# Splitting merged's chunks between the last branch products, with memory's norm behind them

## The reference

```python
def first_block(x, ...):
    h = rmsnorm(x, norm_pre[l])
    u = h @ w_in[l]
    branches = (gdn_branch(...), gla_branch(...), ssd_branch(...), nsa_branch(...))
    gates = jax.nn.sigmoid(_cols(u, offs, 'merge_gate', 'merge_gate')).reshape(bsz, s_len, N_BRANCH, D_MODEL)
    merged = jnp.zeros((bsz, s_len, D_MODEL), F32)
    for n, y in enumerate(branches):
        merged = merged + gates[:, :, n] * (y @ w_br[l, n].astype(F32))
    out = merged.astype(x.dtype) @ w_out[l]
    x = x + rmsnorm(out, norm_post[l])
    return x

def second_block(x, mem, ...):
    ...
    x = x + memory_cross_attention(rms_norm(x, norm_mem_w[l]), rms_norm(mem, norm_memkv_w[l]),
                                   w_mq[l], w_mkv[l], mem_q_norm_w[l], mem_k_norm_w[l], w_mo[l])
```

## Time and profile before

| | us |
|---|---|
| median of 3 runs | 1944.07 |
| lowest, highest | 1939.2, 1944.46 |
| the profiled execution | 1942.46 |
| its span in the profile | 1939.4 |
| PE busy | 1863.8 |
| VectorE, ScalarE, POOL busy | 820.2, 662.7, 534.0 |
| mean granted clock of TensorE | 0.99 of 2.4 GHz |

### The profile page before, as it was taken

The page is one execution under the profiler, slowest core; times in us unless marked ns, Lnnn a source line. Parts: engine busy times, 40 slices in busy tenths (PEclk is TensorE's granted clock), DMA queues, the critical chain, the costliest instruction groups (busy, mean ns, idle before and its releaser), DMA issues. The chain is left out here.

```text
span 1939.4 us, 29067 instructions
## 1 busy us (share of the span) xinstructions
PE 1863.8 (96%) x11709; PEld 1370.5 (71%) x11709; DVE 820.2 (42%) x1692; ACT 662.7 (34%) x1417; POOL 534.0 (28%) x412
## 2 busy tenths in 40 slices
PE   6999999999999999998999998999999999999997
PEld 5789988888898666676878876987774444444443
DVE  4466565344322555533423255323343444333333
ACT  4543233332223555543343256444331111111110
POOL 2342143435543444273245231353200000000000
PEclk9999999999999999999999999999999999999999
DMA  5230122213132211152223221223529999999994
GB/s 165 67 91 25 45 61 93 75 44 109 55 96 82 74 34 44 44 202 98 85 87 107 69 97 23 88 87 116 211 94 378 414 415 413 421 423 417 420 423 173
DMA packets 132681, 313.40 MB, mean 162 GB/s; under 512 B 15280, under 2 KB 102080, under 8 KB 107968
## 3 DMA queue, kind: packets, MB, share of 16 engines
q1 hardware_dynamic: 132544, 311.49, 43.1%
HBM read 309.37 MB, written 2.10 MB: 161 GB/s over the span
## 5 line engine op out<-in xcount | busy, mean ns | idle before, releaser
L321 POOL TENSOR_TENSOR unit_low<-unit_ring,unit_high 128x512 fp32r<-128x512 f32 x332 | 437.3, 1342 | 771.6 <-ACT unit_high L314 771.5
L358 PE MATMUL dense<-hT,unit_high 128*128 128x512 f32 x560 | 228.8, 409 | 3.0 <-DVE dense_temps L531 1.7
L360 PE MATMUL dense<-hT,unit_low 128*128 128x512 f32 x560 | 219.7, 392 | 0.0
L359 PE MATMUL dense<-hT,unit_high 128*128 128x512 f32 x560 | 219.5, 392 | 0.0
L314 ACT CAST unit_high<-unit_ring 128x512 fp32r<-128x512 f32 x332 | 186.2, 618 | 32.3 <-PE dense L360 22.0
L451 PE MATMUL dense<-unit_high,hT 128*128 128x256 f32 x608 | 176.0, 289 | 0.7 <-POOL unit_low L321 0.4
L452 PE MATMUL dense<-unit_low,hT 128*128 128x256 f32 x608 | 172.0, 283 | 0.0
L453 PE MATMUL dense<-unit_high,hT 128*128 128x256 f32 x608 | 171.9, 283 | 0.0
L4295 DVE TENSOR_TENSOR x<-x,side 128x512 f32<-128x512 f32 x128 | 80.6, 682 | 115.5 <-PE side L4137 115.5
L358 PEld LDWEIGHTS dense<-hT,unit_high 128*128 128x128 f32 x560 | 106.0, 189 | 29.1 <-issue 3.6
L359 PEld LDWEIGHTS dense<-hT,unit_high 128*128 128x128 f32 x560 | 106.1, 190 | 23.6 <-issue 3.1
(11 more groups left out here) (606 smaller groups left out, 3642.2 us busy)
## 6 DMA issues: line engine op xcount, KB each, us to landing
expert_slot<-w_exp_gate SPq DMA_DIRECT2D x64, 1024.0 KB, 10.3
expert_slot<-w_exp_up SPq DMA_DIRECT2D x64, 1024.0 KB, 10.6
expert_slot<-w_exp_down SPq DMA_DIRECT2D x64, 1024.0 KB, 9.6
unit_ring<-w_in SPq DMA_DIRECT2D x55, 1024.0 KB, 5.2
unit_ring<-w_mkv SPq DMA_DIRECT2D x8, 1024.0 KB, 5.4
unit_ring<-w_br SPq DMA_DIRECT2D x14, 512.0 KB, 6.4
x<-x SPq DMA_DIRECT2D x8, 512.0 KB, 5.7
w_out_raw<-w_out SPq DMA_DIRECT2D x4, 1024.0 KB, 9.4
```

The costliest lines, as they stand in the source:

```text
L321: nc.gpsimd.tensor_tensor(low[:, at:at + 512], raw[:, at:at + 512], high[:, at:at + 512], ALU.subtract).then_inc(*self.split.up())
L358: nc.tensor.matmul(out, high[:, k, c], rh, start=(k == 0), stop=False)
L359: nc.tensor.matmul(out, high[:, k, c], rl, start=False, stop=False)
L360: last = nc.tensor.matmul(out, low[:, k, c], rh, start=False, stop=(k == kd - 1))
```

## The change

A new function `split_merged` holds one split of `merged`, as it stood in `output_projection`. It is now called from `blocks`: splits 0 and 1 ahead of product 4, 2 and 3 ahead of product 5, 4 ahead of product 6, 5 ahead of product 7, and 6 and 7 behind it. Memory's norm is written behind all eight. The load of `mix_gain` moves behind the reload of x on SP. Of the weights' rests, those whose number i is no multiple of three go to VectorE (ten of sixteen; POOL keeps 0, 3, 6, 9, 12 and 15), where the odd ones went before. Product 3 and gate 6 are written earlier between the pieces, product 3 ahead of piece 11 and not 12, gate 6 ahead of piece 13 and not behind the loop. PE's own order doesn't change.

```diff
+def split_merged(core, S, merged, k):
...
+        if k == 0:
+            act.wait_ge(*S.last_gate)
+        act.wait_ge(*S.merged_chunk[k])
+        nc.scalar.mul(hT[:, 0, k, :], merged[:, k, :], 0.5).then_inc(*scalars.up())
+    high = scalars.now()
...
+        dve.wait_ge(*high)
+        nc.vector.scalar_tensor_tensor(out=hT[:, 1, k, :], in0=merged[:, k, :], scalar=0.5, in1=hT[:, 0, k, :],
+                                       op0=ALU.mult, op1=ALU.subtract).then_inc(*vectors.up())
+    S.split[k] = vectors.now()
...
-def output_projection(core, ring, S, x, xin, merged, gain_row, w_high, w_low, temps, turn_memory, mem_keys):
+def output_projection(core, ring, S, x, xin, gain_row, w_high, w_low, temps, turn_memory, mem_keys, load_mix_gain):
...
-    for k in range(KD):
...
-            nc.scalar.mul(hT[:, 0, k, :], merged[:, k, :], 0.5).then_inc(*scalars.up())
...
-            nc.vector.scalar_tensor_tensor(out=hT[:, 1, k, :], in0=merged[:, k, :], scalar=0.5, in1=hT[:, 0, k, :],
-                                           op0=ALU.mult, op1=ALU.subtract).then_inc(*vectors.up())
-        split[k] = vectors.now()
...
     again = [s.now() for s in S.x_sems]
+    load_mix_gain()
...
-            if i in (0, 2, 5, 8, 12):
-                next(dense, None)
+            if i in (0, 2, 5, 8, 11, 13):
+                next(dense)
...
-            if i % 2:
+            if i % 3:
...
-        next(dense)
         wait_for(section.sync, [S.yT_ready, S.held_free[1]])
...
+        next(dense)
+
+        for chunks in ((0, 1), (2, 3), (4,), (5,)):
+            for k in chunks:
+                split_merged(core, S, merged, k)
+            next(dense)
         run(dense)
+        for k in (6, 7):
+            split_merged(core, S, merged, k)
         wait_for(section.scalar, [S.held_free[7]])
...
-        wait_for(section.sync, mem_ready[1:])
-        S.mix_gain_landed = load("mix_gain", (S.mix_gain[:], ins["norm_mix_w_2"].to_broadcast([P, D])))
...
+        def load_mix_gain():
+            wait_for(section.sync, mem_ready[1:])
+            S.mix_gain_landed = load("mix_gain", (S.mix_gain[:], ins["norm_mix_w_2"].to_broadcast([P, D])))
```

More of the change, by code:

```diff
@@ L775, in __init__ @@
         self.chunk, self.conv_out_free, self.merged_chunk, self.pool_chunk = {}, {}, {}, {}
+        self.split = {}
         self.reduced, self.x_done, self.root_ready, self.mem_heads_done = {}, {}, {}, {}
@@ L2383, in first_norm, with _ @@
     S.hT_ready = vectors.now()
-def output_projection(core, ring, S, x, xin, merged, gain_row, w_high, w_low, temps, turn_memory, mem_keys):
+def split_merged(core, S, merged, k):
+    nc, section, hT = core.nc, core.section, S.hT
+    vectors, scalars = core.sig("core_vectors"), core.sig("core_scalars")
+    @section.scalar
+    def _(act):
+        if k == 0:
[3 more added lines that the diff above has]
+    high = scalars.now()
+    @section.vector
+    def _(dve):
+        dve.wait_ge(*high)
[3 more added lines that the diff above has]
+def output_projection(core, ring, S, x, xin, gain_row, w_high, w_low, temps, turn_memory, mem_keys, load_mix_gain):
     nc = core.nc
@@ L2393, in output_projection @@
     rs = S.head_sums
-    last_gate, split = S.last_gate, {}
+    split = S.split
     part = S.out_part
@@ L2815, in blocks @@
         mem_keys = dense_mem_k(core, ring, S, memT, kT_mem)
-        output_projection(core, ring, S, x, xin, merged, post_gain, w_high, lambda k: w_low[:, k, :], temps, turn_memory, mem_keys)
+        def load_mix_gain():
+            wait_for(section.sync, mem_ready[1:])
+            S.mix_gain_landed = load("mix_gain", (S.mix_gain[:], ins["norm_mix_w_2"].to_broadcast([P, D])))
+        output_projection(core, ring, S, x, xin, post_gain, w_high, lambda k: w_low[:, k, :], temps, turn_memory, mem_keys, load_mix_gain)
         block_two(core, ring, S, x, place, load, temps, mem_keys, memT, kT_mem, route, route_landed, experts)
```

## The result

The changed kernel takes 1929.01 us, median of five runs from 1924.61 to 1931.44; before took 1943.7 in five runs beside them. The ratio is 0.9925, 95% interval 0.9913 to 0.9937: 14.7 us faster. The profiled execution of after has a span of 1925.6 us, 13.8 under that of before.

What follows compares the result with a forecast made beforehand. PE, busy 96% of 1939.4 us, bounds the kernel, so gains come from its waits. Terms of 4.9 and 8.7 make 13.6 us, taken from 1942.46 and 1944.07: 1928.9 and 1930.5, said 1929.5; range 1924 to 1936.

Steps and rivals of the forecast that it cites:

- First term: Rests moved from POOL to VectorE: wait before product 4 falls to 1.8 us, product 5 starts 4.9 us earlier.
- Second term: Splits between products 4 to 7, ahead of memory's norm: projection waits about 1.1 us at full clock; 8.7 us gained.
- The half-speed starts: Matmuls behind the waits before product 4 and the output projection start at half clock, costing 2.4 and 2.3 us.
- Memory's norm: Written behind split 7, its first tile is ready at about 886.0, wanted at 890.5: hidden, 4.5 us of cover.
- SP: SP's queue: reload of x, now ahead of mix_gain, stays hidden, and mix_gain is in time; both cost 0.
- The rule that was weighed: VectorE instructions with two SBUF inputs and GpSimd ones exclude each other: gain 13.6 us with it, 14.0 without.
- (a): Rival: the clock falls in the wait left before product 4; 2.4 us less, 11.2 gained, about 1932; chance 0.13.
- (b): Rival: no wait stays before product 4, POOL reaching the rest by 865.5; 15.6 us gained, about 1927.5; chance 0.13.
- (c): Rival: VectorE late, read of product 5 beyond 875.8, product 7 and gate 6 wait; some 10.5 us gained; chance 0.09.
- (d): Rival: splits' chain slower than PE, waits move into products 5 to 7; gain under 5.8 us, about 1939; chance 0.05.
- (e): Rival: memory's norm behind all eight splits holds the transposes past 904.06; slower than before, above 1944; chance 0.02.
- I take 1 to 1: Behind 904 PE's few waits move along with other engines' work, so the gain reaches the end in full.

Runs made afterwards that it cites:

- Part 1 alone: Kernel before with ten rests on VectorE, product 3 ahead of piece 11, gate 6 ahead of piece 13: 1942.09 us, 0.9997 of before; repeats 0.9994 and 0.9994.
- part 2 alone: Changed kernel with rests, product 3 and gate 6 put back as before; splits between products 4 to 7 and norm behind them stay: 0.9961 of before.

## Why the prediction was right

**First term, 4.9 us.** POOL reached the first rest 20.8 us after its start, where the prediction had 865.9 - 845.04 = 20.9. The price for the thirteen instructions that stay, 1.25 alone and 1.74 beside VectorE's, was right, and so was their mix. Before, eight of sixteen were short and eight long; after, three are short and ten long (1.47 and 1.60 on average), which is the prediction's three short ones less and two held by 0.5 more. The wait was 1.78 (said 1.8), the clock stayed, and the second rest held product 4 for 0.25 us (said 0.3). Start of product 5, counted from PE's being free: 1.78 + 2.73 + 0.25 = 4.8, said 4.8. The bound "868.8", for 5% more on all thirteen, should be 868.3 (5% of 20.9 is 1.0); nothing else hangs on it.

**Second term, 8.7 us.** The projection started 1.00 us behind product 7, said 1.1, released by VectorE's read as said, and no split was late. Both terms: 13.4 us measured on the stretch, 13.6 said. Alone they gave 5.7 (4.5 in one of three profiles) and 8.5 against 4.9 and 8.7. Part 1 alone saves 0.3 more, since without splits between the products nothing holds the second rest, and its second half-speed start was 0.7 us shorter in two of three profiles and 0.5 longer in one; part 2 alone had a longer first wait and a shorter half-speed start, which nearly cancel.

**The half-speed starts.** 2.4 and 2.3 were reckoned, 4.7 together; matmuls in the waits gave 4.5.

**Memory's norm.** The first tile was ready at 887.5, wanted at 892.39: cover 4.9, said 4.5. **SP.** The reload of x was issued some 15.8 us ahead of its add and caused no wait:

```profile
884.06 1.90 SPq L2424 DMA_DIRECT2D x<-x  x4
```

```profile
899.84 1.23 DVE L2497 TENSOR_TENSOR x<-x,out_part 128x1024 f32<-128x1024 f32 x1 [0.25 <-DVE out_part L2484]
```

`mix_gain` was issued at 889.0, landed 5.4 us later and was first read at 902.8, so it cost nothing either.

**At the start of the expert stage.** The prediction wanted the 13.6 us there unchanged. From PE's being free behind gate 7 to the first expert's matmuls the two profiles of before have 582.9 and 580.3 us, the two of after both 567.1: 14.5 less on the mean, with 2.6 between two executions of one kernel.

**The rule that was weighed.** Splits and POOL's rests hold each other: two splits took 2.54 us in the midst of POOL's work (868.61), where eight took 4.89 before, and two of POOL's rests 2.98, where 1.25 is one alone. By the Trainium skill, "SBUF — State Buffer", section "SBUF: two separate sides", they exclude each other; the 0.3 us for which product 4 is held, and which neither part 1 alone nor the kernel with all splits behind product 7 has (10.78 and 10.77 for products 4 to 7 against 11.05), agree with it.

**The rivals.** (a) The clock didn't fall at 1.78 us. It stayed in the wait of 2.07 with the norm ahead of two splits, and fell in that of 3.64 with eight rests on VectorE; what lies between no run here shows. (b) A wait stayed. Its condition was put 1.25 us too late: with a first rest that only starts at 865.5, PE would still wait some 1.3 us. (c), (d) PE waited for nothing inside products 5 to 7, and in product 4 only for the 0.25. VectorE's read of product 5, the tightest place of the chain, ended at 876.40, and product 7 wanted its bank at 877.61: 1.2 us to spare, where the prediction's own times leave 0.6 (875.8 against 874.5 + 0.69) and not its 0.9. Gate 6 didn't wait either. (e) The norm wasn't late.

**Where it was right by less than it seemed.** "I take 1 to 1" is true of the full-clock part. Of the 13.6 us, 4.7 are clock, and the runs of the other kernels show that such a gain may be lost again elsewhere: for part 1 alone the expectation was 4.9 us, and its 34 runs are on average 1.1 us under before. With both parts it arrived whole. The prediction looked only at the waits behind the stretch and not at the clock there, so this part of the hit is luck as far as is known. The range of 1924 to 1936 holds all eleven runs of after (1924.6 to 1935.3).

## What to carry to other kernels

Look at what each engine's queue has in front of the instruction that PE waits for: two long waits went away here without one instruction less, by moving eight splits and a norm past each other and three instructions out of POOL's way. Price a wait as its idle time plus the half-speed start behind it, but count only the idle time as certain: here the clock's share was lost again with part 1 alone, in falls at places that the change doesn't touch. To compare versions a few us apart, read the same stretch between the same two instructions, and set span times mean granted clock beside the medians.

## What was not expected of the hardware

- The granted clock stayed at 1.00 behind waits of PE of 1.62, 1.65 and 2.07 us after dense matmuls, and fell to 0.50 behind 3.64, 4.33, 5.24 and 7.35. Behind waits of 1.64 and 0.51 us in the memory attention, amid small matmuls, it fell in one profile of before and not in the other. At the start of the program the same wait went both ways: 3.20 us at 20.03 in before with the 24 matmuls behind it in 5.73 us, and 2.62 in after with 7.33:

```profile
20.05 7.33 PE L2222 MATMUL dense<-hT,w_small_split 128*56 128x512 f32 x24 [2.62 <-DVE hT L2374]
```

- Falls in unchanged code come in equal amounts: between 1300 and 1460, in all fourteen profiles, the clock's part is 0, 3.4, 5.1 or 6.9 us, multiples of 1.7. The clock's part of the whole program is 19.8 us in before and 11.6 in after. It, more than the work, makes the runs of one kernel differ: in the 80 runs of before it has a standard deviation of 3.0 us, span times clock one of 1.1 (1917.8 to 1922.5), where the runs took 1936.7 to 1948.1.
- Half speed behind the 7.5 us wait did not last equally long: the projection's 48 matmuls took 12.50, 12.51, 13.13, 13.17 and 13.70 us in five profiles.
